# GpSimd multiplies the sparse attention's probabilities by gate and inverse sum; VectorE keeps maxima, reciprocals and copies

## Chip, cores and metric

One Trainium2 chip, one core. The metric is the device time of one execution in microseconds (us).

## What is computed

A decoder trunk of two layers on 256 tokens of width 1024: a sparse attention layer, a differential attention layer, a convolutional gated FFN behind each, a last norm. The change lies in the sparse attention alone. Cut to what matters:

```python
s_s = jnp.einsum('bqkgd,bqknjd->bqkgnj', qrb, k_sel) * scale
p_s = masked_softmax(s_s, m_s[:, :, :, None], axis=(-2, -1))
o_s = jnp.einsum('bqkgnj,bqknjd->bqkgd', p_s, v_sel)
s_w = jnp.einsum('bqkgd,bwkd->bqkgw', qrb, kwb) * scale
p_w = masked_softmax(s_w, m_w[None, :, None, None, :])
o_w = jnp.einsum('bqkgw,bwkd->bqkgd', p_w, vwb)
o = gb[..., 0:1] * o_c + gb[..., 1:2] * o_s + gb[..., 2:3] * o_w
```

There are 16 query heads on 4 key heads. With 256 tokens the selected blocks are all blocks and the window holds all tokens, so both branches are causal attention over up to 256 keys, each with keys and values of its own. The gate and the inverse of the softmax sum of a row are one factor for each query, head and branch, and the kernel multiplies the exponentials by it before P times V, so that both branches add up in one PSUM bank.

## The kernel before

Every engine has its own program, in the order written by hand, and the engines meet at semaphores only. Products of float32 are made from high and low parts, so most weights pass ScalarE (high part, L881) and VectorE (low part, L1239: stage minus high part) before TensorE uses them. GpSimd computes the first and third norm's reciprocal roots in small dependent steps and, late, the scaling of some attention heads.

**The ring.** The sparse attention works in 16 units u = (g, t, m2): key head g, query tile t of 128 tokens, and m2, one of two pairs of heads. A unit has four score tiles, two heads e by two branches y, of 128 queries by (t + 1) x 128 keys; units 0, 1, 4, 5, 8, 9, 12, 13 have t = 0 (128 keys), the others t = 1 (256 keys). Scores lie in `psA` (two slots by u % 2), exponentials in `probs` in the arena (two slots), their transposes in `psT` (both banks belong to one unit) and `pT`. The stages of a unit:

- TensorE, `nsa_scores(u)`: q times k (L606), causal mask (L610).
- VectorE, `maxima(u)`: negated row maxima from PSUM (L1483).
- ScalarE, `exps(u)`: four exponentials with row sums into `den` (L1076).
- VectorE, `scale_probs(u)`: reciprocal of the sums (L1488), factor from reciprocal and gate (L1506, 128x4), four products in place (L1512). `reciprocals` also waits for its own result, since the factor reads it next.
- TensorE, `nsa_transpose(u)` (L623), which waits for the four products and for both copies of unit u - 1.
- ScalarE copies bank 0 (L1093), VectorE bank 1 (`copy_pT`, L1520).
- TensorE, `nsa_pv(w, y)` (L638), w = u // 2: branch 0 of a pair of units in one turn, branch 1 with the compressed branch (L643) in the next.
- ScalarE and VectorE split the result into high and low parts (L1099, L1495).

The order in the steady part is, on TensorE, for u from 4:

```python
if u + 2 < len(UNITS):
    nsa_scores(u + 2)
nsa_transpose(u)
nsa_pv(u // 2 - 1, u % 2)
```

and on VectorE:

```python
maxima(u + 2, ((u + 2) // 2) % 2, "")
scale_probs(u + 1)
copy_pT(u)
if u % 2 == 0:
    oT_lo(u // 2 - 2)
if u in (7, 9, 11, 13):
    split(C_WO + (u - 7) // 4, ((u - 7) // 2 % 2,))
```

Units 0 to 3 are interleaved with the compressed branch: the phi products (L660), its small products on VectorE (L1528 to L1537), the compressed scores (L651) and their softmax (L1549 to L1567). Behind the ring TensorE goes on with the output projection (`out_project`, L364 to L366).

## Time and profile before

| | |
|---|---|
| three runs | 690.19, 692.16, 692.38 us, median 692.16 |
| profiled execution | 689.63 us, its span 687.3 us |
| busy over the span | TensorE 94%, VectorE 74%, ScalarE 60%, GpSimd 2% (13.1 us) |
| chain that ended last | TensorE 76%, VectorE 14%, ScalarE 4% |
| ring of the sparse attention | about 81 to 148 us, in the slices 5 to 9 of 40 |

The span runs from the first instruction of the core to the last. Busy times count the records of an engine; records of successive instructions overlap a little, so the step from one start to the next is the cost of an instruction in a full engine.

### The profile page before, as it was taken

How to read it: one execution, taken by the hardware profiler on the slowest of the kernel's cores; microseconds unless marked ns; L12 is line 12 of the kernel's file. 1: busy time of each engine (PE TensorE's matmuls, PEld its weight loads, DVE VectorE, ACT ScalarE, POOL GpSimd, SP SyncE). 2: the span in 40 equal slices, each digit the busy share in tenths (PEclk: the TensorE clock that was granted, in tenths of full speed). 3: DMA queues.
4: the chain of work that ended last, by engine and by line, in shares of the span. 5: the costliest groups of instructions: out<-in, count | busy, mean ns of one | idle time of the engine just before them, and what ended most of it. 6: DMA issues, size and time to landing. Idle time of an engine off the chain costs nothing.

```text
span 687.3 us, 10853 instructions
## 1 busy us (share of the span) xinstructions
PE 643.0 (94%) x3634; PEld 537.0 (78%) x3634; DVE 509.7 (74%) x967; ACT 414.7 (60%) x839; POOL 13.1 (2%) x49
## 2 busy tenths in 40 slices
PE   5999988989899999999998999869899999999994
PEld 4998776568788888888887888557788888888893
DVE  4378479945888888888877545895688888878885
ACT  5454457735766666666657454664766666666654
POOL 0200000000000000000002000020000000000000
PEclk9999999999999999999999999999999999999998
DMA  7665130116344555555532545222455555555511
GB/s 270 210 236 203 53 123 2 62 62 226 113 185 184 190 199 202 203 191 194 195 126 80 205 161 184 107 93 67 180 185 185 184 184 191 194 199 192 194 70 61
DMA packets 20479, 108.98 MB, mean 159 GB/s; under 512 B 2529, under 2 KB 2913, under 8 KB 11361
## 3 DMA queue, kind: packets, MB, share of 16 engines
q1 hardware_dynamic: 20448, 108.58, 43.7%
q8 instruction: 19, 0.31, 0.2%
q14 instruction: 12, 0.09, 0.0%
HBM read 107.52 MB, written 1.05 MB: 158 GB/s over the span
## 4 chain that ended last, share of the span: by engine, by line
PE 76%; DVE 14%; ACT 4%; issue 2%; DMA 2%; POOL 1%; SPq 0%; POOLq 0%; DVEq 0%; ACTq 0%
PE psA L364 12%; PE psA L365 12%; PE psA L366 12%; PE psO L465 10%; PE psT L465 10%; PE psO L469 6%; PE psT L469 6%; DVE win_lo L1239 3%; DVE stat L1483 2%; DMA stage<-in_w_group 2%; DVE arena L1512 2%; ACT arena L1076 1%; ACT arena L903 1%; DVE arena L1520 1%; DVE win_lo L1320 1%
## 5 line engine op out<-in xcount | busy, mean ns | idle before, releaser
L1320 DVE TENSOR_TENSOR win_lo<-stage,win_hi 128x1024 fp32r<-128x1024 f32 x90 | 109.4, 1219 | 5.7 <-ACT win_hi L933 5.7
L1337 DVE SCALAR_TENSOR_TENSOR arena<-arena,prm 128x255 f32<-128x255 f32 (+1 forms) x152 | 73.5, 484 | 53.8 <-ACT arena L959 51.1
L465 PE MATMUL psO<-hA,win_hi 128*128 128x512 f32 x304 | 109.4, 399 | 0.0
L465 PE MATMUL psT<-hA,win_hi 128*128 128x512 f32 x304 | 108.5, 397 | 0.0
L933 ACT ACTIVATE win_hi<-stage 128x1024 fp32r<-128x1024 f32 x92 | 96.2, 1052 | 11.0 <-PE psA L366 6.4
L469 PE MATMUL psO<-hA,win_lo 128*128 128x256 f32 x336 | 94.4, 281 | 0.0
L469 PE MATMUL psT<-hA,win_lo 128*128 128x256 f32 x336 | 94.3, 281 | 0.0
L1239 DVE TENSOR_TENSOR win_lo<-stage,win_hi 128x1024 fp32r<-128x1024 f32 (+3 forms) x62 | 69.6, 1159 | 31.7 <-ACT win_hi L881 31.4
L959 ACT ACTIVATE arena<-arena,prm 128x256 f32<-128x256 f32 x76 | 45.6, 600 | 55.1 <-DVE arena L1343 54.9
L881 ACT ACTIVATE win_hi<-stage 128x1024 fp32r<-128x1024 f32 (+3 forms) x60 | 57.6, 1005 | 28.6 <-PE psA L366 19.5
L364 PE MATMUL psA<-wout_hi,act_hi 128*128 128x512 f32 x176 | 69.4, 394 | 0.6 <-DVE act_lo L1386 0.5
L365 PE MATMUL psA<-wout_lo,act_hi 128*128 128x512 f32 x176 | 69.0, 392 | 0.0
L366 PE MATMUL psA<-wout_hi,act_lo 128*128 128x512 f32 x176 | 68.5, 389 | 0.0
L465 PEld LDWEIGHTS psO<-hA,win_hi 128*128 128x128 f32 x304 | 57.1, 188 | 14.3
L465 PEld LDWEIGHTS psT<-hA,win_hi 128*128 128x128 f32 x304 | 57.1, 188 | 13.6
L364 PE MATMUL psA<-win_hi,hA 128*128 128x512 f32 (+3 forms) x160 | 61.0, 381 | 5.1 <-DVE win_lo L1239 4.6
L469 PEld LDWEIGHTS psT<-hA,win_lo 128*128 128x128 f32 x336 | 63.5, 189 | 1.4
L469 PEld LDWEIGHTS psO<-hA,win_lo 128*128 128x128 f32 x336 | 63.6, 189 | 0.0
L366 PE MATMUL psA<-win_hi,hA 128*128 128x512 f32 (+3 forms) x160 | 59.7, 373 | 0.0
L365 PE MATMUL psA<-win_lo,hA 128*128 128x512 f32 (+3 forms) x160 | 59.7, 373 | 0.0
L1326 DVE TENSOR_TENSOR wout_lo<-stage_out,wout_hi 128x1024 fp32r<-128x1024 f32 x42 | 51.5, 1225 | 0.8
L969 ACT ACTIVATE act_hi<-arena 128x256 fp32r<-128x256 f32 x42 | 17.6, 419 | 55.4 <-DVE arena L1359 55.4
(253 smaller groups left out, 1158.9 us busy)
## 6 DMA issues: line engine op xcount, KB each, us to landing
stage<-in_w_ffn_in SPq DMA_DIRECT2D x44, 1024.0 KB, 5.4
stage_out<-in_w_ffn_out SPq DMA_DIRECT2D x44, 516.0 KB, 3.5
stage<-in_w_kv SPq DMA_DIRECT2D x8, 1024.0 KB, 4.8
stage<-in_w_group SPq DMA_DIRECT2D x5, 1024.0 KB, 5.7
stage<-in_w_nsa_out SPq DMA_DIRECT2D x4, 1024.0 KB, 5.2
stage<-in_w_dq SPq DMA_DIRECT2D x4, 1024.0 KB, 4.7
stage<-in_w_dout SPq DMA_DIRECT2D x4, 1024.0 KB, 4.8
stage<-in_w_phi SPq DMA_DIRECT2D x2, 1024.0 KB, 5.1
```

Source lines behind the costliest of these rows:

```text
L364: mm(out, xh, wh, start=start, stop=False)
L365: mm(out, xh, wl, start=False, stop=False)
L366: return mm(out, xl, wh, start=False, stop=stop)
L465: mm(o, win_hi[:, slot, cs], hA[:, k, :, :].rearrange("p a q -> p (a q)"), start=k == 0, stop=False)
L469: last = mm(o[:, 0:S], win_lo[:, slot, cs], hA_hi[:, k, :], start=False, stop=k == KT - 1)
L881: act.activation(win_hi[:, s % 2, cs], stage[:, n % 2, cs], ACT.Copy).then_inc(sem["in_hi"], 1)
L933: act.activation(win_hi[:, slot, h * W // 2:(h + 1) * W // 2], stage[:, slot, h * W // 2:(h + 1) * W // 2], ACT.Copy).then_inc(sem["in_hi" ...
L959: act.activation(conv[:, b, g, :], src, ACT.Identity, bias=prm[:, b, 4 * g + 3:4 * g + 4], scale=prm[:, b, 4 * g + 2:4 * g + 3]).then_inc( ...
L1239: last = dve.tensor_tensor(win_lo[:, s % 2, cs], stage[:, n % 2, cs], win_hi[:, s % 2, cs].bitcast(F32), sub)
L1320: last = dve.tensor_tensor(win_lo[:, slot, cs], stage[:, slot, cs], win_hi[:, slot, cs].bitcast(F32), sub)
L1326: dve.tensor_tensor(wout_lo[:, b, :], stage_out[:, b, 0:D], wout_hi[:, b, :].bitcast(F32), sub).then_inc(sem["out_lo"], 1)
L1337: dve.scalar_tensor_tensor(conv[:, b, g, k:S], src[:, 0:S - k], prm[:, b, 4 * g + 2 - k:4 * g + 3 - k], conv[:, b, g, k:S], ALU.mult, ALU. ...
```

## The change

The factor and the four products move from VectorE to GpSimd. GpSimd goes through the 16 units in order, between its first norm and its third; for each it waits for the reciprocal (`recip`), makes the factor, waits for it, and multiplies. VectorE's `scale_probs` is gone, and where it stood only `reciprocals` is called, which no longer waits for its own result (the differential attention, which uses it too, waits at its call). TensorE and ScalarE have the same programs.

```diff
--- before.py
+++ after.py
@@ -855,6 +855,20 @@
 
             pool.memset(eps, EPS).then_inc(sem["eps_ready"], 1)
             norm(0)
+
+            pool.wait_ge(sem["gates_ready"], 1)
+            for u in range(KVH * TT * 2):
+                g, t, m2 = u // 4, (u // 2) % 2, u % 2
+                h0 = 2 * (2 * g + m2)
+                pool.wait_ge(sem["recip"], u + 1)
+                pool.tensor_tensor(fac[:, u, :].rearrange("p (e y) -> p e y", e=2), rec[:, u, :].rearrange("p (e y) -> p e y", e=2),
+                                   gates[:, t, h0:h0 + 2, 1:3], ALU.mult).then_inc(sem["factor"], 1)
+                pool.wait_ge(sem["factor"], u + 1)
+                for e in range(2):
+                    for y in range(2):
+                        pr_ = probs[:, u % 2, e, y, 0:(t + 1) * P]
+                        pool.tensor_scalar(pr_, pr_, fac[:, u, 2 * e + y:2 * e + y + 1], None, ALU.mult).then_inc(sem["scaled_p"], 1)
+
             norm(2)
 
             heads_rstd(pool, 0, "sub0_step", "sub0_rstd", fused=False)
@@ -1486,7 +1500,6 @@
             def reciprocals(u, pre):
                 dve.wait_ge(sem[pre + "probs"], 4 * (u + 1))
                 dve.reciprocal(rec[:, u, :], den[:, u, :]).then_inc(sem[pre + "recip"], 1)
-                dve.wait_ge(sem[pre + "recip"], u + 1)
 
             NU = KVH * TT * 2
             def oT_lo(w):
@@ -1496,21 +1509,6 @@
                                   hB_hi[:, 2 * g:2 * g + 2, t * P:(t + 1) * P].bitcast(F32), sub).then_inc(sem["oT_lo"], 2)
 
 
-            dve.wait_ge(sem["gates_ready"], 1)
-
-            def scale_probs(u):
-
-                g, t, m2 = u // 4, (u // 2) % 2, u % 2
-                reciprocals(u, "")
-                h0 = 2 * (2 * g + m2)
-                dve.tensor_tensor(fac[:, u, :].rearrange("p (e y) -> p e y", e=2), rec[:, u, :].rearrange("p (e y) -> p e y", e=2),
-                                  gates[:, t, h0:h0 + 2, 1:3], ALU.mult).then_inc(sem["factor"], 1)
-                dve.wait_ge(sem["factor"], u + 1)
-                for e in range(2):
-                    for y in range(2):
-                        pr_ = probs[:, u % 2, e, y, 0:(t + 1) * P]
-                        dve.tensor_scalar(pr_, pr_, fac[:, u, 2 * e + y:2 * e + y + 1], None, ALU.mult).then_inc(sem["scaled_p"], 1)
-
             def copy_pT(u):
 
                 m2, nb = u % 2, (u // 2) % 2 + 1
@@ -1521,8 +1519,8 @@
 
             maxima(0, 0, "")
             maxima(1, 0, "")
-            scale_probs(0)
-            scale_probs(1)
+            reciprocals(0, "")
+            reciprocals(1, "")
 
             dve.wait_ge(sem["phi_used"], N_PHI)
             dve.tensor_tensor(hid, psO[:, 0, 0:PHI], b1, ALU.add).then_inc(sem["hid_z"], 1)
@@ -1541,7 +1539,7 @@
             for e in range(2):
                 dve.tensor_copy(kcT[e * 64:e * 64 + 64, e, :, :].rearrange("p g c -> p (g c)"), psO[e * 64:e * 64 + 64, 0, 0:64]).then_inc(sem["kcmp_ready"], 1)
             maxima(3, 1, "")
-            scale_probs(2)
+            reciprocals(2, "")
 
             bc = [P, TT, HEADS, CP]
             dve.wait_ge(sem["cmp_scores"], 1)
@@ -1553,7 +1551,7 @@
             dve.tensor_tensor(cmp_s, cmp_s, cmx.unsqueeze(3).to_broadcast(bc), sub).then_inc(sem["cmp_shift"], 1)
             copy_pT(2)
             maxima(4, 0, "")
-            scale_probs(3)
+            reciprocals(3, "")
 
             dve.wait_ge(sem["cmp_exp"], 1)
             dve.tensor_reduce(csum, cmp_p, AX.X, ALU.add).then_inc(sem["cmp_sum"], 1)
@@ -1567,14 +1565,13 @@
             dve.tensor_tensor(cmp_p, cmp_p, cfac.unsqueeze(3).to_broadcast(bc), ALU.mult).then_inc(sem["cmp_p"], 1)
             copy_pT(3)
             maxima(5, 0, "")
-            scale_probs(4)
+            reciprocals(4, "")
 
             for u in range(4, NU):
                 if u < NU - 2:
                     maxima(u + 2, ((u + 2) // 2) % 2, "")
                 if u < NU - 1:
-
-                    scale_probs(u + 1)
+                    reciprocals(u + 1, "")
                 copy_pT(u)
                 if u % 2 == 0:
                     oT_lo(u // 2 - 2)
@@ -1627,6 +1624,7 @@
 
                 nk = (u % TT + 1) * P
                 reciprocals(u, "d")
+                dve.wait_ge(sem["drecip"], u + 1)
                 dve.scalar_tensor_tensor(fac[:, u, 0:2], den[:, u, 0:2], neg_lam, rec[:, u, 2:4], ALU.mult, ALU.mult).then_inc(sem["dfactor"], 1)
                 dve.wait_ge(sem["dfactor"], u + 1)
                 for e in range(2):
```

VectorE's queue before, around the turns of units 8 and 9 (L1483 maxima, L1488 reciprocal, L1506 factor, L1512 products, L1520 copy, L1239 weight split, L1495 low part of the output):

```order
L1483 TENSOR_REDUCE stat<-psA 128x4
L1488 RECIPROCAL stat<-stat 128x4
L1506 TENSOR_TENSOR stat<-stat,gates 128x4
L1512 TENSOR_SCALAR arena<-arena,stat 128x128 x4
L1520 COPY arena<-psT 128x4x128
L1239 TENSOR_TENSOR win_lo<-stage,win_hi 128x1024
L1483 TENSOR_REDUCE stat<-psA 128x4
L1488 RECIPROCAL stat<-stat 128x4
L1506 TENSOR_TENSOR stat<-stat,gates 128x4
L1512 TENSOR_SCALAR arena<-arena,stat 128x128 x4
L1520 COPY arena<-psT 128x2x128
```

These are the maxima of unit 9 and the products of unit 8, the copy of unit 7 and the split, then the maxima of unit 10, the products of unit 9 and the copy of unit 8.

The same stretch of VectorE's queue in the change (L1497 maxima, L1502 reciprocal, L1518 copy, L1253 weight split):

```order
L1497 TENSOR_REDUCE stat<-psA 128x4
L1502 RECIPROCAL stat<-stat 128x4
L1518 COPY arena<-psT 128x4x128
L1253 TENSOR_TENSOR win_lo<-stage,win_hi 128x1024
L1497 TENSOR_REDUCE stat<-psA 128x4
L1502 RECIPROCAL stat<-stat 128x4
L1518 COPY arena<-psT 128x2x128
```

The factor and the products have left; the reciprocal still stands behind the maxima of the unit after its own.

GpSimd's queue in the change, from the end of its first norm (L250) on (L864 factor, L870 products):

```order
L250 TENSOR_TENSOR stat<-stat 128x2
L864 TENSOR_TENSOR stat<-stat,gates 128x4
L870 TENSOR_SCALAR arena<-arena,stat 128x128 x4
L864 TENSOR_TENSOR stat<-stat,gates 128x4
L870 TENSOR_SCALAR arena<-arena,stat 128x128 x4
L864 TENSOR_TENSOR stat<-stat,gates 128x4
L870 TENSOR_SCALAR arena<-arena,stat 128x256 x4
```

Each factor waits for its unit's reciprocal and each first product for its factor; the pattern goes on to unit 15, and the third norm stands behind it.

## Rows read from the trace of the kernel before

**Rows 1.** Busy time by window: us, busy us (instructions) of each engine, clock, DMA.
```profile
117.64:131.20 13.56, 11.98 (x105) 7.86 (x106) 13.28 (x37) 11.88 (x43) 0.00 (x0) 1.00 0.13 40
...
144.06:148.33 4.27, 4.27 (x45) 3.42 (x45) 1.30 (x3) 0.98 (x2) 0.00 (x0) 1.00 0.45 184
```
**Rows 2.** Chain that ended last, from 118 to 146 us, shares by line.
```profile
by line: DVE arena L1512 26.0%; DVE stat L1483 22.6%; DVE win_lo L1239 16.2%; DVE arena L1520 13.4%; DVE stat L1506 5.0%; issue 4.3%; PE psT L623 3.8%; DVE hB_lo L1495 3.6%; DVE stat L1488 2.7%; PE psO L638 2.1%; PE psO L643 1.1%; DVEq L149
```
**Rows 3.** Timeline of VectorE, 101 to 113 us: start, us, engine, line, form, count [idle].
```profile
101.35 0.17 DVE L1488 RECIPROCAL stat<-stat 128x4 f32<-128x4 f32 x1
...
103.91 0.20 DVE L1563 TENSOR_TENSOR stat<-stat,gates 128x32 f32<-128x32 f32 x1
...
104.98 0.68 DVE L1520 COPY arena<-psT 128x512 f32<-128x512 f32 x1
...
111.73 1.23 DVE L1483 TENSOR_REDUCE stat<-psA 128x4 f32<-128x1024 f32 x1 [1.00 <-PE psA L610]
112.87 0.17 DVE L1488 RECIPROCAL stat<-stat 128x4 f32<-128x4 f32 x1
```
**Rows 4.** Timeline of VectorE, one unit's turn and a weight split.
```profile
117.64 0.68 DVE L1483 TENSOR_REDUCE stat<-psA 128x4 f32<-128x512 f32 x1
118.24 0.17 DVE L1488 RECIPROCAL stat<-stat 128x4 f32<-128x4 f32 x1
118.44 0.16 DVE L1506 TENSOR_TENSOR stat<-stat,gates 128x4 f32<-128x4 f32 x1
118.64 0.88 DVE L1512 TENSOR_SCALAR arena<-arena,stat 128x128 f32<-128x128 f32 x4
119.43 0.69 DVE L1520 COPY arena<-psT 128x512 f32<-128x512 f32 x1
120.03 1.22 DVE L1239 TENSOR_TENSOR win_lo<-stage,win_hi 128x1024 fp32r<-128x1024 f32 x1
```
**Rows 5.** Timeline of TensorE, 108 to 123 us.
```profile
108.35 0.65 PE L638 MATMUL psO<-arena,vals 128*64 128x256 f32 x4 [0.18 <-ACT tokA L1135]
...
110.23 1.14 PE L606 MATMUL psA<-keysT,qrT 64*128 64x256 f32 x8
111.30 0.39 PE L610 MATMUL psA<-cmask,identb 128*128 128x256 bf16 x2
...
114.89 1.07 PE L623 MATMUL psT<-ident,arena 128*128 128x128 f32 x8 [0.34 <-DVE arena L1520]
115.88 0.65 PE L638 MATMUL psO<-arena,vals 128*64 128x256 f32 x4
116.47 0.71 PE L606 MATMUL psA<-keysT,qrT 64*128 64x128 f32 x8
117.11 0.39 PE L610 MATMUL psA<-cmask,identb 128*128 128x256 bf16 x2
...
120.85 0.60 PE L623 MATMUL psT<-ident,arena 128*128 128x128 f32 x4
121.38 1.08 PE L638 MATMUL psO<-arena,vals 128*64 128x256 f32 x8
122.39 1.13 PE L606 MATMUL psA<-keysT,qrT 64*128 64x256 f32 x8
```
**Rows 6.** Timeline of GpSimd, 459 to 465 us.
```profile
459.77 0.20 POOL L244 TENSOR_TENSOR stat<-stat 128x8 f32<-128x8 f32 x1
460.05 0.20 POOL L246 TENSOR_TENSOR stat<-stat 128x8 f32<-128x8 f32 x1
...
463.16 2.04 POOL L270 TENSOR_TENSOR tokB<-tokB,stat 128x512 f32<-128x512 f32 x2
```
**Rows 7.** Timeline of TensorE at the same place.
```profile
465.26 0.66 PE L830 MATMUL psT<-ident,tokB 128*128 128x128 f32 x4 [0.34 <-POOL tokB L270]
```
**Rows 8.** Timeline of GpSimd, 367 us.
```profile
367.18 1.23 POOL L852 TENSOR_SCALAR stat<-stat 128x2 f32<-128x2 f32 x1 [344.52 <-ACT arena L903]
```
**Rows 9.** Timeline of VectorE, 366 us.
```profile
366.00 2.35 DVE L1239 TENSOR_TENSOR win_lo<-stage,win_hi 128x1024 fp32r<-128x1024 f32 x2
```

## The prediction

> **What bounds the kernel now.** I read the busy shares by window first, then the chain of waits, then the timelines of the engines inside the ring. Over the whole span TensorE is the busy engine, but the change touches only the sparse attention, about 81 to 148 us. There VectorE is the full one. Units 8 to 11 take 13.56 us, VectorE is busy 13.28 of them, TensorE 11.98, ScalarE 11.88 (overlapping records), GpSimd 0 [rows 1]. The chain that ended last says the same: the multiplications at L1512 are its largest part, 26.0%, the maxima have 22.6% and the copies 13.4% [rows 2]. From the last transposes to the output projection TensorE runs alone for 4.27 us [rows 1]. Behind 148.33 us TensorE works without a gap, so I count a shift of the ring's end in full.
>
> **What the change takes off VectorE.** For a unit of 128 keys the factor costs 0.20 us (118.44 to 118.64) and the four multiplications 0.79 (118.64 to 119.43) [rows 4]. A unit of 256 keys costs more, so four units lose at least 4 x 0.99 = 4.0 us of the 13.56. If VectorE were all that counted, the ring would gain until TensorE's 11.98 us bound it: 1.6 us for four units. It does not gain that, because the work that leaves is a link between engines, and what is left on VectorE stands in an order that makes the new link wait.
>
> **The new loop.** The queues of the change show it. For an even unit u: GpSimd computes the factor and four products; TensorE then transposes u, does the first half of a P times V, and only then the scores of u+3, which stand behind the transposes in its queue; VectorE takes the maxima of u+3, and only behind them the reciprocal of u+2, since its queue has maxima ahead of reciprocals; that releases GpSimd for u+2. GpSimd idles through all of this, though the exponentials of u+2 can be done. Let a be the step of one GpSimd product of 128x128 and b that of 128x256. The terms:
> - factor and its own wait 0.28, the start-to-start of small dependent GpSimd instructions (459.77 to 460.05) [rows 6]. GpSimd to TensorE 0.06: 463.16 + 2.04 = 465.20, TensorE starts at 465.26 [rows 6, 7].
> - u of 128 keys: transposes 0.53, P times V 1.01 (120.85, 121.38, 122.39), scores of 256 keys to VectorE's start 1.50 (110.23 to 111.73), maxima 1.14 (111.73 to 112.87) [rows 3, 5]; reciprocal 0.17 [rows 4] and a hop of 0.04, which is 111.30 + 0.39 to 111.73 [rows 3, 5]. With 0.28 + 0.06 the turn is 4.73 + 4a.
> - u of 256 keys: transposes 0.99, P times V 0.59 (114.89, 115.88, 116.47), scores 0.64 + 0.39 + 0.04 = 1.07 [rows 5], maxima 0.60 [rows 4], the same 0.21 and 0.34: 3.80 + 4b.
> - unit 4 has more P times V behind it, 1.88 instead of 1.01 (108.35 to 110.23) [rows 5]: 5.60 + 4a.
>
> **Collisions.** GpSimd's first small instruction at 367.18 took 1.23 us and ended at 368.41 [rows 8], where its like take 0.20 [rows 6]. VectorE was then in two weight splits (366.00 to 368.35, 1.17 each) [rows 9]: GpSimd waited for the second to end. The split is an instruction with two operands in SBUF; the Trainium skill (SBUF, "Who interferes with whom") says that such a one and a GpSimd instruction that reads SBUF exclude each other, and by that rule the trace agrees. The ring has four such splits (L1239), and in the new order each comes right behind a reciprocal and a copy, while GpSimd multiplies unit 8, 10, 12 or 14. I price each at 1.17, so 4.68. In the same way the three small two-operand steps of the compressed branch (103.91 to 104.98) [rows 3] cost 1.07 while unit 3 is multiplied. Nothing of this was in the kernel before.
>
> **The sum.** I start at the reciprocal of unit 3, at 101.35 in both. GpSimd starts at 101.35 + 0.17 + 0.04 = 101.56 [rows 3], factor to 101.84, four products 4b, collisions 1.07, hop 0.06, transposes and hop 1.13 (1.07 + 0.06; eight matmuls as at 114.89 [rows 5]): the copy of unit 3 starts at 104.10 + 4b, before at 104.98 [rows 3]. Then copy, maxima, reciprocal, hop 0.60 + 0.60 + 0.21 = 1.41 [rows 4]; unit 4: 5.60 + 4a; units 6 and 10: 7.60 + 8b; units 8 and 12: 9.46 + 8a; units 14 and 15 back to back on GpSimd, then the tail: 0.56 + 8b + 0.06 + 4.27 = 4.89 + 8b; splits 4.68. Total 33.64. The ring ends at 137.74 + 12a + 20b, before at 148.33 [rows 1]. **The difference is 12a + 20b - 10.59.** Break-even is therefore at products of about 0.27 and 0.37 us.
>
> **What a and b are.** No row shows this operation on GpSimd. The nearest large one is the product of two tensors, 128x512, 1.02 us each (463.16, two in 2.04), the nearest small one 0.20 at 8 columns [rows 6]: 0.82 / 504 = 1.63 ns a column. Taken in full: a = 0.40, b = 0.60, difference +6.2. If time goes by operands read, the slope is halved, since here one tensor is read and not two: a = 0.30, b = 0.40, +1.0. At the floor of 0.20 for both: -4.2. The shapes lie nearer to the 128x512 row in kind, but the operand count speaks for the lower slope, so I take the middle of the two slopes, **a = 0.35, b = 0.50: 4.2 + 10.0 - 10.6 = +3.6 us**. The Trainium skill (GPSIMD Engine Reference, "4.1 Engine selection") advises against exactly this move: elementwise work belongs on VectorE, GpSimd being about twice as slow with two inputs and roughly at line rate with one; line rate at the page's 1.2 GHz, an estimate of 0.83 ns a column over the same 0.20, would make the sum about +1.3. No row here tests that one-input figure.
>
> Edits at nothing: VectorE's own wait behind its reciprocal goes, 0.03 us a unit, which would show only where VectorE is full; GpSimd's later duties (367 and 459 us) come long after the ring; no DMA is moved, SP's queue is the same. For the first two units the products end by 101.35 in any case, covered by the second phi half, which stands ahead of the transposes of unit 0 on TensorE: 0.28 + 4 x 0.35 = 1.7 us against 0.99 now. If that cover is too short, the difference of 0.7 shows once.
>
> The profiled execution took 689.63 us (span 687.3), so it would become 693.2; the median of the three runs is 692.16, so I forecast **695.8**. A change within 0.3%, 2.1 us, I count as the same.
>
> **Rivals.**
> 1. *GpSimd at the lower slope.* Everything else as above: +1.0, 693.2, not told from no change. For it: one operand. Against it: a per-partition factor must be fetched too. Chance 0.23.
> 2. *The collisions don't fall on the loop* (faster). If the split, which nobody waits for soon, is what waits, and GpSimd finishes its burst first, then 4.68 + 1.07 = 5.75 drop out, and at my a and b the sum is -2.2, 690.0. It decides at about a third of the collision price: with under 2.2 of the 5.75 paid the ring is even. With the lower slope too it would be -4.8 by the sum, but TensorE's 11.98 in four units [rows 1] then binds, so about -3.5. For it: the split is issued when GpSimd is already in a burst. Against it: 367.18, where GpSimd was the one to wait [rows 8]. Chance 0.16, of it 0.13 faster.
> 3. *GpSimd is the engine that bounds.* If a product costs more than the full slope says (say 0.50 and 0.80), four units take 4 x 0.28 + 8 x 0.50 + 8 x 0.80 = 11.5 us of GpSimd plus two splits: +11.4, 703.6. Chance 0.10.
> 4. *The dependency order is looser than I walked it*, for instance since the reciprocal comes early enough, and VectorE's freed 4 us show: down to TensorE's bound, 1.6 us a group over 2.5 groups, about -4. Chance 0.06.
> That the change doesn't do what it says is excluded: its queues show the 16 factors and 64 products on GpSimd.
>
> **How the numbers follow.** The forecast case, +2.1 to +7, has 0.45. Slower by over 0.3%: 0.45 + 0.10 + a part of rival 1, 0.03 = 0.58. Same: the rest of rival 1, 0.20, and 0.03 of rival 2 = 0.23. Faster: 0.13 + 0.06 = 0.19. The range goes from 690.0 (rival 2 at my prices) to 702.0 (products between the full slope and rival 3); outside it lie the best of rivals 2 and 4 and the worst of rival 3, together some 0.15.
>
> **What would show it.** In the changed profile: GpSimd busy some 32 us in the ring, idle before each even unit's factor with VectorE's reciprocal as the releaser; TensorE waiting for GpSimd's products, not for VectorE; VectorE with idle time before maxima, released by TensorE; four products near VectorE's splits that take about 1.5 us instead of 0.4; 14 us between the transposes of unit 8 and 12. I am wrong if products take under 0.3 and 0.4 us (start to start), or if no product is stretched beside a split, or if VectorE is still the full engine. TensorE's granted clock should stay at its upper level (1.00 in the ring's second half [rows 1]); a fall there would add to the loss.

## The result and the profile after

| | before | after |
|---|---|---|
| median of 4 runs | 692.18 us (690.19 to 692.38) | 710.84 us (707.11 to 712.56) |
| profiled execution, span | 689.63, 687.3 | 711.01, 709.1 |
| mean granted clock of TensorE | 0.990 | 0.970 |
| first matmul of the output projection | 148.26 | 169.51 |

The ratio of the medians is 1.028, with a 95% interval of 1.0253 to 1.0308. The change makes the kernel slower by 18.7 us, against a forecast of 3.6: the sign is right, the time lies 9 us above the range. The whole loss lies in the sparse attention. There the first matmul of the output projection (L364), from where TensorE works without a gap, comes 21.25 us later, and the spans differ by 21.8.

The page of the changed kernel, first the busy shares and then the chain that ended last, by engine and by line:

```profile
PE 655.0 (92%) x3634; PEld 545.8 (77%) x3634; DVE 493.2 (70%) x887; ACT 414.7 (58%) x839; POOL 67.2 (9%) x129
...
PE 78%; DVE 9%; POOL 6%; ACT 3%; DMA 2%; issue 2%; SPq 0%; DVEq 0%; ACTq 0%; POOLq 0%
PE psA L364 12%; PE psA L365 11%; PE psA L366 11%; PE psO L465 10%; PE psT L465 10%; PE psO L469 6%; PE psT L469 6%; POOL arena L870 5%; DVE win_lo L1253 2%; DVE stat L1497 2%; PE psT L623 2%; DMA stage<-in_w_group 2%; PE psO L638 1%; PE psA L606 1%; ACT arena L917 1%
```

VectorE has 70% of the span and 9% of the chain. GpSimd is busy for only 9%, and 6% of the chain is its own. That is the change in two lines: a little-used engine became a link. Around the ring, the chain of waits from 98 to 170 us, by line, says so more strongly. It answers to [rows 2], where VectorE's L1512, L1483 and L1239 led:

```profile
by line: POOL arena L870 40.4%; PE psT L623 15.8%; PE psO L638 12.8%; PE psA L606 9.1%; DVE stat L1497 7.7%; PE psO L643 3.6%; PE psA L610 3.1%; POOL stat L864 2.3%; issue 2.2%; DVE arena L1518 1.9%; DVE stat L1502 0.8%; PE psA L364 0.6%
```

GpSimd's products (L870) are 40.4%, the transposes that wait for them 15.8%, P times V (L638) 12.8%, the scores (L606) 9.1%, the maxima (L1497) 7.7%. No split and hardly a copy is in it. These are the stations of the loop that the prediction walked. Waits of each engine from 80 to 172 us (engine, line waited for: us in total, times, longest):

```profile
POOL stat L864 <- DVE stat L1502: 84.8, 11, 61.1
...
DVE arena L1518 <- PE psT L623: 23.2, 10, 4.9
...
PE psT L623 <- POOL arena L870: 18.9, 11, 4.3
DVE stat L1497 <- PE psA L610: 12.4, 12, 1.6
```

TensorE stands still for 18.9 us before its transposes, in waits of up to 4.3 us, and VectorE waits for it in turn. The timeline of GpSimd over the steady part (start, us, line, form, count, idle time before and its releaser):

```profile
118.39 0.20 POOL L864 TENSOR_TENSOR stat<-stat,gates 128x4 f32<-128x4 f32 x1 [2.80 <-DVE stat L1502]
118.69 3.63 POOL L870 TENSOR_SCALAR arena<-arena,stat 128x256 f32<-128x256 f32 x4
...
122.59 3.63 POOL L870 TENSOR_SCALAR arena<-arena,stat 128x256 f32<-128x256 f32 x4
...
127.10 2.35 POOL L870 TENSOR_SCALAR arena<-arena,stat 128x128 f32<-128x128 f32 x4
133.20 0.20 POOL L864 TENSOR_TENSOR stat<-stat,gates 128x4 f32<-128x4 f32 x1 [3.75 <-DVE stat L1502]
...
136.04 0.20 POOL L864 TENSOR_TENSOR stat<-stat,gates 128x4 f32<-128x4 f32 x1 [0.19 <-DVE stat L1502]
136.34 4.41 POOL L870 TENSOR_SCALAR arena<-arena,stat 128x256 f32<-128x256 f32 x4
...
153.92 0.20 POOL L864 TENSOR_TENSOR stat<-stat,gates 128x4 f32<-128x4 f32 x1 [1.55 <-DVE stat L1502]
```

Four products of 128x128 take 2.35 us and four of 128x256 take 3.63 when nothing disturbs them. So a = 2.35 / 4 = 0.59 and b = 3.63 / 4 = 0.91, not 0.35 and 0.50. GpSimd is idle before most of the factors, for VectorE's reciprocal (L1502): 2.80 us before unit 6, 3.75 before unit 9. Units 6 and 7 run back to back (118.69, 122.59). Unit 10 (136.34) is stretched to 4.41. Units 10 to 13 take 153.92 - 136.04 = 17.88 us, against 13.56 for four units before. In windows (us, busy us of PE, PEld, DVE, ACT and POOL, granted clock, DMA):

```profile
136.04:153.92 17.88, 14.92 (x116) 9.79 (x117) 9.41 (x17) 11.26 (x42) 14.33 (x21) 0.90 0.16 59
104.00:106.00 2.00, 0.00 (x0) 0.00 (x0) 1.04 (x2) 0.97 (x6) 2.00 (x4) 1.00 0.00 0
124.00:130.00 6.00, 5.64 (x32) 3.83 (x30) 3.03 (x6) 4.17 (x18) 4.76 (x8) 0.50 0.01 1
158.00:168.00 10.00, 8.30 (x40) 5.77 (x42) 2.14 (x4) 1.58 (x3) 4.57 (x6) 0.50 0.14 56
```

VectorE is busy 9.41 us of 17.88, and was 13.28 of 13.56 [rows 1]. TensorE is idle for whole windows (104 to 106) and at other places works at a granted clock of 0.50, the lower of its levels (1.2 GHz), where both windows of [rows 1] had 1.00. Its timeline at two such places answers to [rows 5]:

```profile
122.37 1.09 PE L623 MATMUL psT<-ident,arena 128*128 128x128 f32 x8 [2.55 <-POOL arena L870]
...
124.13 1.23 PE L606 MATMUL psA<-keysT,qrT 64*128 64x128 f32 x8
...
126.27 1.97 PE L623 MATMUL psT<-ident,arena 128*128 128x128 f32 x8 [0.36 <-POOL arena L870]
...
158.82 1.97 PE L623 MATMUL psT<-ident,arena 128*128 128x128 f32 x8 [4.29 <-POOL arena L870]
```

The eight transposes at 126.27 take 1.97 us, against 1.07 at 114.89 [rows 5]. The kernel before has a short stretch at this level as well, ahead of its steady part:

```profile
98.00:100.00 2.00, 2.00 (x10) 1.71 (x8) 0.95 (x2) 0.00 (x0) 0.00 (x0) 0.50 0.00 0
```

In the changed kernel that stretch is there too (window 98:102: 0.50), and TensorE does not wait for GpSimd ahead of it: it is busy for all of the ten us from 90 to 100. The later ones, from 107 us on, come after its waits.

### The profile page after: what moved, and what is told of

It is laid out like the page before. It is cut to its first block, busy times and chain, and to the rows that moved or that the text cites. A ratio compares the mean times of both kernels' runs of the same rounds, so it can differ in the third digit from the quotient of the medians.

```text
span 709.1 us, 10853 instructions
## 1 busy us (share of the span) xinstructions
PE 655.0 (92%) x3634; PEld 545.8 (77%) x3634; DVE 493.2 (70%) x887; ACT 414.7 (58%) x839; POOL 67.2 (9%) x129
## 4 chain that ended last, share of the span: by engine, by line
PE 78%; DVE 9%; POOL 6%; ACT 3%; DMA 2%; issue 2%; SPq 0%; DVEq 0%; ACTq 0%; POOLq 0%
PE psA L364 12%; PE psA L365 11%; PE psA L366 11%; PE psO L465 10%; PE psT L465 10%; PE psO L469 6%; PE psT L469 6%; POOL arena L870 5%; DVE win_lo L1253 2%; DVE stat L1497 2%; PE psT L623 2%; DMA stage<-in_w_group 2%; PE psO L638 1%; PE psA L606 1%; ACT arena L917 1%
## 5 line engine op out<-in xcount | busy, mean ns | idle before, releaser
L1253 DVE TENSOR_TENSOR win_lo<-stage,win_hi 128x1024 fp32r<-128x1024 f32 (+3 forms) x62 | 69.8, 1161 | 32.5 <-ACT win_hi L895 32.2
L364 PE MATMUL psA<-wout_hi,act_hi 128*128 128x512 f32 x176 | 69.4, 394 | 0.6 <-DVE act_lo L1400 0.5
L364 PE MATMUL psA<-win_hi,hA 128*128 128x512 f32 (+3 forms) x160 | 60.9, 381 | 4.7 <-DVE win_lo L1253 4.1
L870 POOL TENSOR_SCALAR arena<-arena,stat 128x128 f32<-128x128 f32 (+1 forms) x64 | 50.6, 808 | 1.6
```

Of the source, the lines that this page charges most:

```text
L364: mm(out, xh, wh, start=start, stop=False)
L870: pool.tensor_scalar(pr_, pr_, fac[:, u, 2 * e + y:2 * e + y + 1], None, ALU.mult).then_inc(sem["scaled_p"], 1)
L1253: last = dve.tensor_tensor(win_lo[:, s % 2, cs], stage[:, n % 2, cs], win_hi[:, s % 2, cs].bitcast(F32), sub)
```

## Experiments

All times are medians, each against runs of the kernel before on the same chip. What an edit gave is told by the differences to these: the changed kernel stands at +18.7. "Ring end" is the start of the first matmul of the output projection in the profiled execution, 148.26 before. Behind it 539 to 541.5 us follow in every kernel, so that a shift there counts nearly in full. The four runs of the changed kernel lie 5.5 us apart (707.11 to 712.56), so a difference of 2 to 4 us between the medians of two experiments is near the noise. For such differences the traces are read as well, from GpSimd's factor of unit 3 to the ring's end, which takes 169.51 - 102.88 = 66.63 us in the changed kernel.

| kernel | us | before | ratio, 95% | ring end |
|---|---|---|---|---|
| after | 710.84 | 692.18 | 1.028 (1.0253 to 1.0308) | 169.51 |
| immediate | 704.73, one run | 692.00 | | 163.20 |
| warm | 706.62 | 692.00 | 1.0221 (1.0184 to 1.0258) | 164.79 |
| recip_first | 707.34 | 692.00 | 1.0234 (1.0192 to 1.0276) | 165.01 |
| no_split | 707.32 | 690.71 | 1.0244 (1.0215 to 1.0273) | 164.12 |
| recip_first_warm | 704.98 | 691.03 | 1.0209 (1.0184 to 1.0234) | 162.55 |
| four_two_tensor | 696.43 | 690.48 | 1.0079 (1.0051 to 1.0106) | 155.88 |
| one_product | 692.83 | 692.00 | 1.0016 (0.9989 to 1.0042) | 152.16 |
| one_product_recip_first | 691.63 | 690.71 | 1.0018 (1.0000 to 1.0036) | 146.59 |
| factor_only | 690.74 | 690.71 | 1.0014 (0.9993 to 1.0035) | 149.00 |
| odd_units | 690.83 | 690.71 | 0.9997 (0.9982 to 1.0013) | 149.89 |
| middle_units | 689.94 | 691.03 | 0.9987 (0.9969 to 1.0004) | 146.48 |
| before_recip_first | 700.37 | 691.03 | 1.0152 (1.0129 to 1.0176) | 156.45 |

My theory after the result: the products themselves, at 2.5 ns a column, are most of the loss, the loop passes them on one for one, and the collisions, the clock and the order add the rest. Rivals: the clock is the main cause; the collisions are; the handover between engines is.

### One product in place of four

```diff
-                for e in range(2):
-                    for y in range(2):
-                        pr_ = probs[:, u % 2, e, y, 0:(t + 1) * P]
-                        pool.tensor_scalar(pr_, pr_, fac[:, u, 2 * e + y:2 * e + y + 1], None, ALU.mult).then_inc(sem["scaled_p"], 1)
+                pr_ = probs[:, u % 2, :, :, 0:(t + 1) * P]
+                pool.tensor_tensor(pr_, pr_, fac[:, u, :].rearrange("p (e y) -> p e y", e=2).unsqueeze(3).to_broadcast([P, 2, 2, (t + 1) * P]),
+                                   ALU.mult).then_inc(sem["scaled_p"], 4)
```

> The changed kernel, but GpSimd makes one product of two tensors for a unit (probabilities 128x512 or 128x1024 times the factor, repeated along the keys) in place of four products with a per-partition factor. Theory A, the form is what is slow (0.585 and 0.905 us a product in the changed kernel, 2.5 ns a column, where the two-tensor product of the heads' scaling took 1.63): a unit takes about 1.04 and 1.9 us in place of 2.35 and 3.63, the clock no longer falls in the second half of the ring, and the kernel takes 690 to 695 us. Theory B, GpSimd's time goes by columns whatever the form: 2.3 and 3.6 us a unit, 711 us.

Measured: 692.83 us, +0.8, not told from the kernel before. From GpSimd's timeline:

```profile
121.79 1.04 POOL L868 TENSOR_TENSOR arena<-arena,stat 128x512 f32<-128x512 f32 x1
...
128.10 0.20 POOL L864 TENSOR_TENSOR stat<-stat,gates 128x4 f32<-128x4 f32 x1 [1.45 <-DVE stat L1501]
128.44 2.77 POOL L868 TENSOR_TENSOR arena<-arena,stat 128x1024 f32<-128x1024 f32 x1
...
131.52 1.90 POOL L868 TENSOR_TENSOR arena<-arena,stat 128x1024 f32<-128x1024 f32 x1
...
141.46 0.20 POOL L864 TENSOR_TENSOR stat<-stat,gates 128x4 f32<-128x4 f32 x1 [1.45 <-DVE stat L1501]
```

The same multiplications take 1.04 us (128x512, the price of [rows 6] to 0.02) and 1.9 us (128x1024), where four with a scalar take 2.35 and 3.63. Unit 10 to unit 14 takes 141.46 - 128.10 = 13.36 us, as long as a group did before. So the handover and the order stand as they were, and the 18.7 us are gone: they hung on what the products take, directly and through what follows from it. (The profiled execution took 694.65 us, 1.8 above the median, so its ring ends later than the median lets expect.) At 128.44 the product is stretched from 1.9 to 2.77, beside VectorE's split at 128.25.

### The scalar from the instruction

```diff
-                        pool.tensor_scalar(pr_, pr_, fac[:, u, 2 * e + y:2 * e + y + 1], None, ALU.mult).then_inc(sem["scaled_p"], 1)
+                        pool.tensor_scalar(pr_, pr_, 0.5, None, ALU.mult).then_inc(sem["scaled_p"], 1)
```

> The changed kernel with the constant 0.5 as the factor of the four products, so the factor isn't applied to the probabilities (the output is another one). Prices the per-partition factor. Theory A, fetching the factor from memory is what costs 2.5 ns a column against 1.63 for a two-tensor product: the products fall below 0.41 and 0.62 us, the kernel below 700. Theory B, a product of a tensor with a scalar has this speed on GpSimd by itself: 0.585 and 0.905 us as before, 711 us.

Measured: 704.73 us in one run, between the two expectations. The timeline of GpSimd:

```profile
112.69 2.02 POOL L870 TENSOR_SCALAR arena<-arena 128x128 f32<-128x128 f32 x4
...
117.29 3.29 POOL L870 TENSOR_SCALAR arena<-arena 128x256 f32<-128x256 f32 x4
...
133.80 4.22 POOL L870 TENSOR_SCALAR arena<-arena 128x256 f32<-128x256 f32 x4
```

A product takes 2.02 / 4 = 0.505 and 3.29 / 4 = 0.82 us: the slope is (0.82 - 0.505) / 128 = 2.5 ns a column as before, and the pointer to the scalar costs 0.08 us an instruction, not more. The slope belongs to the form, one tensor with a scalar, wherever the scalar comes from. That is 32 x 0.08 = 2.6 us by the prediction's terms, and the one run came 6 us lower. Its trace says where the rest is to be looked for: from the factor of unit 14 to the ring's end it takes 163.20 - 150.85 = 12.35 us at a mean granted clock of 0.86, the changed kernel 169.51 - 153.92 = 15.59 us at 0.67. Of these 3.2 us the eight products explain 0.6. So TensorE's clock fell for less of the ring here, and one run can't say how much of that is the edit's doing.

### The two-tensor form, still four instructions

```diff
-                        pool.tensor_scalar(pr_, pr_, fac[:, u, 2 * e + y:2 * e + y + 1], None, ALU.mult).then_inc(sem["scaled_p"], 1)
+                        pool.tensor_tensor(pr_, pr_, fac[:, u, 2 * e + y:2 * e + y + 1].to_broadcast([P, (t + 1) * P]), ALU.mult).then_inc(sem["scaled_p"], 1)
```

> The changed kernel with its four products a unit, each written as a product of two tensors (the factor repeated along the keys) and not of a tensor and a per-partition factor. Separates the form from the number of instructions. Theory A, the form has the slope: 0.40 and 0.60 us a product (0.20 and 1.63 ns a column) in place of 0.585 and 0.905; 1.6 and 2.4 us a unit, the ring by the sum of the prediction at plus 6.2 less the collisions that were priced too high: 694 to 699 us. Rival, four instructions cost what they cost in either form and only the single instruction is cheap: 2.3 and 3.6 us a unit, 708 to 711.

Measured: 696.43 us, +5.95. From GpSimd's timeline, four of 128x128 and four of 128x256 undisturbed, and one of each stretched:

```profile
112.90 1.47 POOL L870 TENSOR_TENSOR arena<-arena,stat 128x128 f32<-128x128 f32 x4
...
117.02 2.32 POOL L870 TENSOR_TENSOR arena<-arena,stat 128x256 f32<-128x256 f32 x4
...
123.21 2.45 POOL L870 TENSOR_TENSOR arena<-arena,stat 128x128 f32<-128x128 f32 x4
...
130.48 3.26 POOL L870 TENSOR_TENSOR arena<-arena,stat 128x256 f32<-128x256 f32 x4
```

With the same number of instructions on the same data, the form alone is worth 18.7 - 5.95 = 12.7 us; going from four instructions to one is worth 5.1 more. A product takes 1.47 / 4 = 0.37 and 2.32 / 4 = 0.58 us, 1.7 ns a column, which is the full slope of the prediction's [rows 6]. The prediction's formula gives 12 x 0.37 + 20 x 0.58 - 10.59 = +5.4 for it, 0.6 us from the measured. Part of that is luck. The formula holds 5.75 us for collisions, of which 0.98, 0.94, 0.98 and 0.95 are paid here at units 8, 10, 12 and 14, and nothing for the clock, which stood at 0.50 from 96 to 100 and from 106 to 110 us; and the ring's end moved by 7.6 us.

### The clock

```diff
-                pe_.wait_ge(sem["scaled_p"], 4 * (u + 1))
...
+                for _ in range({3: 24, 4: 12, 6: 20, 7: 6, 9: 10, 10: 14, 12: 8, 14: 34, 15: 16}.get(u, 0)):
+                    mm(psT[:, 1, 0:S], hA_hi[:, 0, 0:P], hA_hi[:, 0, :], start=True, stop=True)
+                pe_.wait_ge(sem["scaled_p"], 4 * (u + 1))
```

> The changed kernel with 144 extra matmuls (256 columns, result unused, about 0.11 us each) on TensorE ahead of the transposes of units 3, 4, 6, 7, 9, 10, 12, 14 and 15, where it waited 0.9 to 4.3 us for GpSimd. GpSimd's work is unchanged. Theory A, the idle waits let the clock fall to 1.2 GHz (granted 0.50 at 98-103, 107-110, 124-130, 141-144 and 158-168 us), and this costs about 7 us on the chain: transposes of 1.97 us go back to 1.07, the granted clock stays at 1.00, the kernel takes 703 to 705 us. Rival, the low clock is hidden behind GpSimd: 710 to 712 us.

Measured: 706.62 us. TensorE fills its waits for GpSimd with matmuls that nobody reads. Its timeline and two windows:

```profile
119.66 2.63 PE L619 MATMUL psT<-hA 128*128 128x256 f32 x20
122.46 1.09 PE L625 MATMUL psT<-ident,arena 128*128 128x128 f32 x8 [0.17 <-POOL arena L872]
...
126.34 1.09 PE L625 MATMUL psT<-ident,arena 128*128 128x128 f32 x8 [0.53 <-POOL arena L872]
...
120.00:130.00 10.00, 9.23 (x79) 7.03 (x78) 4.46 (x9) 5.75 (x23) 9.56 (x13) 1.00 0.01 2
...
150.00:160.00 10.00, 9.29 (x78) 7.99 (x78) 3.95 (x7) 3.96 (x12) 8.65 (x11) 1.00 0.30 107
```

From 104 us on, where the first of these matmuls run, the granted clock stays at 1.00 (2.4 GHz), and the transposes take 1.09 us again. The kernel stands at +14.6, 4.0 us lower by the medians, and its time lies between the two expectations. By the traces it is more: from the factor of unit 3 to the ring's end it takes 164.79 - 103.85 = 60.94 us, 5.7 less than the changed kernel, although its products pay 3.2 us beside the splits in place of 2.5 (3.21 for unit 8, 4.14, 3.28 and 4.55). So the low clock costs some 4 to 6 us in the ring, and the 7 us added up from the stretched pieces of the chain were not far off.

### The order on VectorE

```diff
             for u in range(4, NU):
-                if u < NU - 2:
-                    maxima(u + 2, ((u + 2) // 2) % 2, "")
                 if u < NU - 1:
                     reciprocals(u + 1, "")
+                if u < NU - 2:
+                    maxima(u + 2, ((u + 2) // 2) % 2, "")
```

> The changed kernel with VectorE's reciprocal of unit u+1 ahead of its maxima of unit u+2 for u from 4. Theory A, the order makes GpSimd idle (2.8, 3.8, 1.3, 1.6 us before the factors of units 6, 9, 12, 14) though the exponentials are done: about half of it goes, 4 to 5 us, 706 us, and a bit more if the clock falls less. Rival 1, the exponentials end only then, so nothing is won: 711. Rival 2, the maxima now wait for the exponentials of the unit before, so ScalarE starts later: 712 to 716.

Measured: 707.34 us, +15.3, so 3.3 less by the medians, and 66.63 - (165.01 - 102.62) = 4.2 less by the traces. In one window (columns as above):

```profile
120.00:130.00 10.00, 8.68 (x62) 5.95 (x64) 5.80 (x11) 6.20 (x24) 9.52 (x15) 0.83 0.00 1
```

GpSimd is busy 9.52 us of ten (fifth pair), so at these products it bounds the ring there and the better order can give little. With both edits, clock and order:

> The changed kernel with both the reciprocal ahead of the maxima and the 144 extra matmuls in TensorE's waits. Theory A, order and clock are separate losses and add up (3.5 and 4.2 us): 702.5 to 703.5 on the scale of 710.8 for the changed kernel. Rival, the earlier reciprocal gained mainly because waits and so clock falls got shorter, and the two overlap: 705 to 706.5.

Measured: 704.98 us, +13.95, which is the rival's 706.1 on the scale of the changed kernel. Order and clock alone give 3.3 and 4.0 us by the medians, both together 4.7, not 7.3; by the traces 4.2 and 5.7, together 66.63 - (162.55 - 103.96) = 8.0, not 9.9. Both ways point to an overlap, but it is no larger than the noise of these runs, and its size stays open.

### Without VectorE's splits beside the products

```diff
-                        last = dve.tensor_tensor(win_lo[:, s % 2, cs], stage[:, n % 2, cs], win_hi[:, s % 2, cs].bitcast(F32), sub)
+                    if zero:
+                        last = dve.memset(win_lo[:, s % 2, cs].bitcast(F32), 0.0)
+                    else:
+                        last = dve.tensor_tensor(win_lo[:, s % 2, cs], stage[:, n % 2, cs], win_hi[:, s % 2, cs].bitcast(F32), sub)
...
-                    split(C_WO + (u - 7) // 4, ((u - 7) // 2 % 2,))
+                    split(C_WO + (u - 7) // 4, ((u - 7) // 2 % 2,), True)
```

> The changed kernel, but VectorE's four weight splits inside the ring write zeros (no tensor read) in place of stage minus high part, so the first two chunks of the output projection's weights lose their low parts. Prices the collisions. Theory A, only the stretches seen in the trace count (4.41 against 3.63, 3.17 against 2.35, 4.55 against 3.63: 2.5 us together): 708 us. Theory B, as predicted, all four splits in full, 4.7: 706. Rival, the stretches are hidden: 711.

Measured: 707.32 us, +16.6. The timeline of GpSimd at unit 10, then, of the changed kernel, VectorE's timeline beside units 8 and 10 and the records of the products from 126 to 142 us (ns, shortest, median, longest):

```profile
134.72 3.63 POOL L870 TENSOR_SCALAR arena<-arena,stat 128x256 f32<-128x256 f32 x4
```

```profile
128.88 1.41 DVE L1253 TENSOR_TENSOR win_lo<-stage,win_hi 128x1024 fp32r<-128x1024 f32 x1
...
136.94 1.22 DVE L1253 TENSOR_TENSOR win_lo<-stage,win_hi 128x1024 fp32r<-128x1024 f32 x1
...
L870 POOL TENSOR_SCALAR arena<-arena,stat x15: 604/607/1706, 125.3 to 141.9; 128x128 f32<-128x128 f32 x8, 128x256 f32<-128x256 f32 x7
```

The products that took 4.41 us beside the split at 136.94 take 3.63 when VectorE only writes zeros: the collision is shown. All of it is in one record of 1.71 us, where its like take 0.92. It is smaller than priced. Unit 10 pays 4.41 - 3.63 = 0.78 us, unit 12 0.82, unit 14 0.92 (3.17 and 4.55 us), and unit 8 nothing: there VectorE's split at 128.88 takes 1.41 instead of 1.22. Together that is 2.5 us, and the run stands 2.1 lower, which is within the noise and does not price the collisions by itself: its clock also stayed at 1.00 from 120 to 150 us, where that of the changed kernel fell. The records price them. What a product pays is what is left of the split when it starts, less some 0.14 us: the second product of unit 10 starts at 136.34 + 0.91 = 137.25 and the split ends at 136.94 + 1.22 = 138.16, which leaves 0.91; at one_product's unit 10 128.25 + 1.22 - 128.44 = 1.03 are left and 2.77 - 1.90 = 0.87 are paid.

### The handover alone

```diff
-                pool.wait_ge(sem["factor"], u + 1)
-                for e in range(2):
-                    for y in range(2):
-                        pr_ = probs[:, u % 2, e, y, 0:(t + 1) * P]
-                        pool.tensor_scalar(pr_, pr_, fac[:, u, 2 * e + y:2 * e + y + 1], None, ALU.mult).then_inc(sem["scaled_p"], 1)
...
+            def products(u):
+                dve.wait_ge(sem["factor"], u + 1)
+                for e in range(2):
+                    for y in range(2):
+                        pr_ = probs[:, u % 2, e, y, 0:((u // 2) % 2 + 1) * P]
+                        dve.tensor_scalar(pr_, pr_, fac[:, u, 2 * e + y:2 * e + y + 1], None, ALU.mult).then_inc(sem["scaled_p"], 1)
...
                     reciprocals(u + 1, "")
+                    products(u + 1)
```

> GpSimd computes only the factor (128x4) and VectorE makes the four products, as before, waiting for GpSimd. Prices the two handovers of a unit. Theory A, VectorE idles for factor and hops, about 0.35 us a unit in place of the 0.20 of its own factor, for 10 to 16 units: plus 1.5 to 3 us on the kernel before, 693.5 to 695. Rival, the handovers are covered by other work: 692.

Measured: 690.74 us, no difference: my expectation missed. VectorE waits for the factor 16 times, 5.1 us in all:

```profile
DVE arena L1512 <- POOL stat L864: 5.1, 16, 0.4
...
118.34 0.17 DVE L1497 RECIPROCAL stat<-stat 128x4 f32<-128x4 f32 x1
118.81 0.88 DVE L1512 TENSOR_SCALAR arena<-arena,stat 128x128 f32<-128x128 f32 x4 [0.31 <-POOL stat L864]
```

From the reciprocal's start to the first product 0.47 us pass, 0.40 before (118.24 to 118.64 [rows 4]). The detour costs 0.07 us a unit, since VectorE computes no factor any more. A handover by semaphore is cheap here; what is handed over is dear.

### Versions that could gain

With one product, the order was changed as above:

> One two-tensor product a unit on GpSimd, and VectorE's reciprocal of unit u+1 ahead of its maxima of u+2. With one product GpSimd still idles 1.3 to 3.1 us before a factor, with VectorE's reciprocal as the releaser. Theory A, the order costs here what it did with four products (3.5 us between the two medians): 688.5 to 691. Rival, GpSimd was late there only because it was nearly full, and with short products the exponentials set the time: 692 to 693.5.

Measured: 691.63 us, not the gain expected. In the profiled execution, the fastest of its 12 runs, four units (11 to 15) take 140.05 - 127.25 = 12.8 us and the ring ends at 146.59:

```profile
127.25 0.20 POOL L864 TENSOR_TENSOR stat<-stat,gates 128x4 f32<-128x4 f32 x1 [1.25 <-DVE stat L1501]
127.60 1.90 POOL L868 TENSOR_TENSOR arena<-arena,stat 128x1024 f32<-128x1024 f32 x1
...
140.05 0.20 POOL L864 TENSOR_TENSOR stat<-stat,gates 128x4 f32<-128x4 f32 x1 [1.25 <-DVE stat L1501]
```

It also lacks the low clock at 96 to 100 us that the profile of before has (window 96:100: 1.00, before 0.61). Over its runs, the mean granted clock is 0.992 in the fastest (687.5) and 0.978 to 0.981 in the three slowest (693.3 to 694.6). What sets the clock in an execution was not settled. Then GpSimd took the odd units only, so that its work lies beside VectorE's:

```diff
-            for u in range(KVH * TT * 2):
+            for u in range(1, KVH * TT * 2, 2):
...
+            def products(u):
+                if u % 2:
+                    return
...
                     reciprocals(u + 1, "")
+                    products(u + 1)
```

> GpSimd takes factor and one two-tensor product of the odd units only, VectorE keeps the even ones as before. VectorE then has some 11.3 us in four units in place of 13.56, TensorE 12. Theory A, the ring is set by VectorE's load and TensorE's, and GpSimd's 1.04 and 1.89 us have room: minus 2 to 4 us, 688.5 to 690. Rival, GpSimd's latency (0.3 + 1.89 against 1.26 on VectorE) lies on the chain for the odd units too: 691 to 693.

Measured: 690.83 us, a miss. The timeline of GpSimd:

```profile
116.98 0.20 POOL L867 TENSOR_TENSOR stat<-stat,gates 128x4 f32<-128x4 f32 x1 [5.43 <-DVE stat L1504]
...
130.51 0.20 POOL L867 TENSOR_TENSOR stat<-stat,gates 128x4 f32<-128x4 f32 x1 [5.04 <-DVE stat L1504]
```

Four units take 130.51 - 116.98 = 13.53 us, as before, and GpSimd waits 5 us each time for the reciprocal: that of an odd unit stands on VectorE behind the even unit's products, so that the two engines' products follow each other and don't overlap. Last, GpSimd took the nine units in the middle, reciprocal first, and VectorE the first five and the last two, where GpSimd stands alone in the chain:

```diff
+        G_UNITS = [5, 6, 7, 8, 9, 10, 11, 12, 13]
+        V_UNITS = [0, 1, 2, 3, 4, 14, 15]
...
-            for u in range(KVH * TT * 2):
+            for u in G_UNITS:
...
             for u in range(4, NU):
+                if u + 1 in G_UNITS:
+                    reciprocals(u + 1, "")
                 if u < NU - 2:
                     maxima(u + 2, ((u + 2) // 2) % 2, "")
-                if u < NU - 1:
+                if u < NU - 1 and u + 1 not in G_UNITS:
                     reciprocals(u + 1, "")
+                    products(u + 1)
```

> GpSimd takes units 5 to 13 alone, with one two-tensor product a unit, VectorE's reciprocal of these units ahead of the maxima of the next, and VectorE keeps units 0 to 4, 14 and 15 with their products. In the run with all units on GpSimd and this order the steady part took 12.80 us for four units (factor of unit 10 to factor of unit 14) against 13.56 before, and the loss lay at units 3 and 4 (waits of 2.4 and 1.0 us) and at the end (1.8). Theory A: the steady gain of about 1.9 us stays and the losses go: 0.5 to 3 us faster than the kernel before. Rival, changing over between the engines costs it again: no difference.

Measured: 689.94 against 691.03 us, ratio 0.9987 (0.9969 to 1.0004), the best of all and still not told from the kernel before. (Its ring end of 146.48 is that of the fastest of its 12 runs.)

### The order in the kernel before

```diff
             for u in range(4, NU):
-                if u < NU - 2:
-                    maxima(u + 2, ((u + 2) // 2) % 2, "")
                 if u < NU - 1:
-
                     scale_probs(u + 1)
+                if u < NU - 2:
+                    maxima(u + 2, ((u + 2) // 2) % 2, "")
```

> The kernel before, with VectorE's reciprocal, factor and products of unit u+1 ahead of its maxima of u+2. A control for the order. VectorE is full there, so if load is what counts the order is worth nothing: within 1 us of the kernel before. Rival, later maxima start ScalarE later: 1 to 3 us slower.

Measured: 700.37 us, 9 us slower, far beyond either expectation. The waits from 80 to 160 us, first of this kernel:

```profile
ACT arena L1076 <- DVE stat L1483: 17.5, 11, 2.7
...
DVE stat L1488 <- ACT arena L1076: 9.1, 10, 1.7
```

And of the kernel before:

```profile
ACT arena L1076 <- DVE stat L1483: 5.8, 5, 2.7
...
DVE stat L1488 <- ACT arena L1076: 0.7, 1, 0.7
```

With the scaling first, ScalarE gets its maxima late (17.5 us of waiting instead of 5.8) and VectorE then waits for the exponentials (9.1 us instead of 0.7). The two take turns, and a group takes 135.50 - 119.16 = 16.34 us instead of 13.56. So the order that cost nothing or gained some 3 us with the products on GpSimd costs 9 with them on VectorE. The edits are alike, not the same: here the factor and the products, 1 us and more a unit, go ahead of the maxima together with the reciprocal.

## Why the prediction was right in sign and wrong in size

- **The start: VectorE is full, and what leaves it is a link.** Right. VectorE has 13.28 - 9.41 = 3.9 us less in four units, 4.0 predicted, and nothing came of it.
- **The new loop.** Right, station by station: the chain of the changed kernel is GpSimd, transposes, P times V, scores, maxima, and GpSimd's idle times end with the reciprocal. The handovers were priced well: the factor's step is 0.30 (118.39 to 118.69) against 0.28, the hop to TensorE 122.37 - 122.32 = 0.05 against 0.06, and factor_only shows nothing of them in the total.
- **The term that failed: "What a and b are".** The prediction took the middle between the full slope and half of it, because one tensor is read and not two. The full slope, 1.63 ns a column, was itself right for two tensors (1.7 measured), but the form with a scalar costs 2.5: 0.59 and 0.91 us. Reading one tensor less made it dearer, not cheaper. Put into the prediction's own formula, 12 x 0.59 + 20 x 0.91 - 10.59 gives +14.7 instead of +3.6, which is 11 of the 15 us that the forecast missed. The range failed by this too: its upper end lay between the full slope and rival 3 (0.50 and 0.80), and the true prices lie above even that. GpSimd is busy for 67.2 us in place of 13.1, 54 us more, where some 32 were foreseen. four_two_tensor, whose prices are near the full slope's, stands at +5.95, where the prediction had +6.2 for the full slope, though with errors of the collisions and the clock that cancel.
- **A rule of the Trainium skill.** Its sentence that GpSimd is about twice as slow on two inputs and roughly at line rate on one (GPSIMD Engine Reference, "4.1 Engine selection") is half borne out. To keep the work on VectorE was the right advice here (710.84 against 692.18), and with two tensor inputs of 128x1024 GpSimd's 1.9 us stand against 1.22 of VectorE's split, 1.6 times as long where the skill has about twice. But one input came out slower than two, 2.35 us for four of 128x128 against 1.47, and the +1.3 us that the page's figure gave was far off.
- **Collisions.** The mechanism was right and priced too high: 5.75 us in the prediction, 2.5 in the records, since a product waits for what is left of a split and not for the whole, and the four products of unit 3 took 3.63 as if alone: there VectorE's step at 104.25 (L1565, 128x512) took 0.85 us, where its like took 0.69 before. Rival 2, that the split is what waits, holds for unit 8 only. The Trainium skill (SBUF — State Buffer, "Who interferes with whom") says of VectorE's two-port modes that whoever issues first holds the shared ports for the whole instruction, and of contention in general that the order of issue decides who waits. The second product of unit 10, which waits for the split's end, agrees with it; the split at 136.94 itself does not, which starts 0.3 us before the end of the first product and still takes 1.22.
- **The clock.** The prediction said that it should stay at its upper level and that a fall would add to the loss. It fell, after waits of TensorE for GpSimd of 1.8 to 4.3 us, and besides at 98 to 102 us, ahead of which there is no such wait. The warm run prices the fall from unit 3 on at 4.0 us by the medians and 5.7 by the traces. This is the second term that failed: the sum put the clock at nothing, though its own working has TensorE wait for the 0.28 + 4b = 2.3 us of unit 3.
- **The first three units.** The reciprocal of unit 3, where the sum begins, comes at 102.63 and not at 101.35, 1.3 us later. "If that cover is too short" was true in part. TensorE waits 0.77 and 0.99 us for the products of units 0 and 1 (at 86.29 and 89.33), where before it waited for nothing and 0.57, so about 1.2 us are the cover's, at 4 x 0.59 = 2.35 us of products a unit. Another 0.7 are the clock's: the 32 matmuls of the compressed scores take 4.37 us in place of 3.71. Together that is 1.9, and the reciprocal is only 1.3 us later because this execution reached the ring 0.7 us earlier (the second phi half starts at 81.85, before at 82.55). That the clock alone can do as much is seen in four_two_tensor: its four products take 1.47 us and the cover suffices, yet its compressed scores take 5.39 us and the factor of unit 3 comes at 103.17, later still.
- **Rival 3, GpSimd bounds.** Partly true: units 6 and 7 run back to back, but before unit 9 GpSimd still waits 3.75 us for the loop, and over units 10 to 13 it is busy for 14.33 of 17.88 us. It had +11.4 for products of 0.50 and 0.80, which is the loop's formula; its own load of 11.5 us and two splits of 1.17 is 13.9 in four units, hardly more than the 13.56 of before, and would not have bounded the ring by that much.

From the factor of unit 3 on, the changed kernel can be laid beside the prediction's own terms, with the measured a = 0.59 and b = 0.91 (4a = 2.36, 4b = 3.64) and the collisions as paid. The last column is TensorE's mean granted clock in the stretch:

| from factor to factor | us | by the terms | more | granted clock |
|---|---|---|---|---|
| unit 3 to 4 | 7.45 | 2.88 + 4b = 6.52 | 0.9 | 0.74 |
| 4 to 6 | 8.06 | 5.60 + 4a = 7.96 | 0.1 | 1.00 |
| 6 to 10 | 17.65 | 8.53 + 4a + 4b = 14.53 | 3.1 | 0.81 |
| 10 to 12 | 9.86 | 3.80 + 4b + 0.78 = 8.22 | 1.6 | 0.83 |
| 12 to 14 | 8.02 | 4.73 + 4a + 0.82 = 7.91 | 0.1 | 1.00 |
| 14 to the ring's end | 15.59 | 4.89 + 8b + 0.92 = 13.09 | 2.5 | 0.67 |

Where the clock stayed at its upper level, the terms hold to 0.1 us. The 8.4 us that are more lie in the four stretches in which it fell. In the warm run, at 1.00, units 6 to 10 take 134.37 - 118.48 = 15.89 us: of the 3.1 us 1.8 are the clock's, and 1.4 stay. There the chain that ended last goes through the products of unit 6 and of unit 7, one behind the other, which the walk along one loop does not count.

So the ring's end moved 21.25 us: 1.3 ahead of unit 3, 14.7 by the formula, less 3.2 for the collisions that were not paid, and 8.4 more, of which the clock has some 6 and products back to back on GpSimd have at least 1.4. The split of the rest between the two is not settled by a run.

## What to carry over

A price for an operation on another engine must come from the same form of instruction, with its operands, and from nothing that is merely alike. When no row has it, the range must reach well above the nearest row. Work that leaves a full engine into a link of a ring lengthens the ring by all it takes there: give it away only where the receiving engine does it about as fast as the loop has slack, as one instruction rather than four, and look for what else hangs on the idle time, such as TensorE's clock. Which of two instructions stands first in a queue can be worth 9 us, and an order that costs so much in one kernel need not cost anything once other work has moved.

## What was not expected of the hardware

- GpSimd's multiplication by a scalar of each partition costs 0.27 us and 2.5 ns a column of float32, with a constant 0.19 us and 2.5 ns; with a second tensor, repeated along the row, 1.7 ns a column (four times 128x128 in 1.47 us, four times 128x256 in 2.32), and as one instruction 1.04 us for 512 columns and 1.9 for 1024. VectorE does four of 128x128 in 0.88.
- A split of VectorE beside a GpSimd product stretches one of the two: the product by 0.8 to 1.0 us where it starts early in the split, or the split from 1.22 to 1.41, at 135.43 in one_product to 1.84.
- TensorE at the granted clock 0.50 did eight transposes in 1.97 us instead of 1.07, in stretches that follow its waits for GpSimd, and in one, at 98 to 102 us, that follows none. Filling the waits with idle matmuls gave back 4.0 us by the medians.
